# Order of a TensorE slot in the prompt attention: scores, values of unit n-3, projection piece, turns of unit n-2

## What is computed

```python
def mla_project(h, pos, w_in, q_norm, w_uq, kv_norm, w_uk):
    a = h @ w_in
    cq, ckv, kpe = jnp.split(a, [Q_LORA, Q_LORA + KV_LORA], axis=-1)
    q = (rmsnorm(cq, q_norm) @ w_uq).reshape(B, T, MLA_HEADS, QK_NOPE + QK_ROPE)
    ...
s = einsum(q, k) * MLA_SCALE                      # 16 heads, 96 wide (64 + 32 rotary)
s = jnp.where(kpos[None, :] <= qpos_b[:, None], s, -jnp.inf)
p = jax.nn.softmax(s, axis=-1)
o = p @ v                                         # 64 wide per head, then @ w_o
```

## Time and profile before

| what | value |
|---|---|
| median of 3 runs (lowest, highest) | 1759.67 us (1758.48, 1760.13) |
| the profiled execution, its own time | 1764.47 us |
| its span, first to last instruction | 1762.6 us |
| TensorE matmul busy | 1556.1 us, 88% of the span |
| VectorE, ScalarE, GpSimd busy | 757.0, 514.1, 389.0 us |
| mean granted TensorE clock | 0.92 of full speed |

### The profile page before, as it was taken

One profiled execution on the slowest core, in us unless ns is written; L12 is line 12 of the kernel. 1 busy time (PEld: TensorE's weight loads), 2 busy tenths in 40 slices (PEclk: granted clock), 3 DMA queues, 4 the chain that ended last, 5 costly groups with the idle time before them and its releaser, 6 DMA issues.

```text
span 1762.6 us, 28171 instructions
## 1 busy us (share of the span) xinstructions
PE 1556.1 (88%) x11027; PEld 1386.2 (79%) x11027; DVE 757.0 (43%) x1000; ACT 514.1 (29%) x884; POOL 389.0 (22%) x282
## 2 busy tenths in 40 slices
PE   3778998899995899999999489999976999999995
PEld 3635655666794899999999477778866999999994
DVE  5425665221137433334343744443546434343435
ACT  3125555221123212222122335443433212122221
POOL 4110000000025413223152500000036405050432
PEclk7989999888696899999999689999987999999996
DMA  7200000323020223222223222222220232232211
GB/s 178 87 16 1 1 1 1 81 72 85 2 72 24 72 85 89 88 85 83 83 83 84 62 60 89 77 88 72 83 72 24 86 94 84 85 91 86 83 59 51
DMA packets 210856, 119.99 MB, mean 68 GB/s; under 512 B 22118, under 2 KB 206592, under 8 KB 210784
## 3 DMA queue, kind: packets, MB, share of 16 engines
q1 hardware_dynamic: 206800, 105.73, 21.1%
q0 software_dynamic: 3984, 13.25, 2.3%
HBM read 111.37 MB, written 7.59 MB: 67 GB/s over the span
## 4 chain that ended last, share of the span: by engine, by line
PE 80%; DVE 11%; ACT 6%; issue 2%; POOL 1%; DMA 0%; DVEq 0%; ACTq 0%; POOLq 0%
PE ps L1523 56%; PE ps L1784 2%; DVE y L1109 2%; PE ps L1662 2%; DVE act_lo L1100 2%; PE ps L1547 2%; PE ps L1760 2%; PE ps L1746 1%; DVE rstd_post L1095 1%; PE ps L1698 1%; PE ps L1621 1%; POOL ssum L619 1%; PE ps L1762 1%; PE ps L1561 1%; DVE x L1114 1%
## 5 line engine op out<-in xcount | busy, mean ns | idle before, releaser
L724 ACT CAST w_hi<-w_raw 128x1024 fp32r<-128x1024 f32 x172 | 180.6, 1051 | 780.6 <-PE ps L1523 771.3
L1523 PE MATMUL ps<-act_hi,w_hi 128*128 128x280 f32 (+1 forms) x1504 | 319.9, 294 | 17.0 <-DVE w_lo L1090 14.2
L1523 PE MATMUL ps<-act_hi,w_lo 128*128 128x280 f32 (+1 forms) x1504 | 317.4, 292 | 0.0
L1523 PE MATMUL ps<-act_lo,w_hi 128*128 128x280 f32 (+1 forms) x1504 | 316.3, 292 | 0.0
L1090 DVE TENSOR_TENSOR w_lo<-w_raw,w_hi 128x1024 fp32r<-128x1024 f32 x172 | 254.9, 1482 | 47.5 <-ACT w_hi L724 45.6
L1523 PEld LDWEIGHTS ps<-act_hi,w_hi 128*128 128x128 f32 x1504 | 240.9, 191 | 23.3 <-DVE w_lo L1090 15.4
L1523 PEld LDWEIGHTS ps<-act_hi,w_lo 128*128 128x128 f32 x1504 | 241.3, 191 | 0.0
L1523 PEld LDWEIGHTS ps<-act_lo,w_hi 128*128 128x128 f32 x1504 | 240.2, 190 | 0.0
L1523 PE MATMUL ps<-h_hi,w_lo 128*128 128x280 f32 (+1 forms) x1024 | 213.7, 290 | 0.0
L1523 PE MATMUL ps<-h_hi,w_hi 128*128 128x280 f32 (+1 forms) x1024 | 212.9, 289 | 0.0
L1523 PE MATMUL ps<-h_lo,w_hi 128*128 128x280 f32 (+1 forms) x1024 | 212.7, 289 | 0.0
(11 more groups left out here) (294 smaller groups left out, 1961.0 us busy)
## 6 DMA issues: line engine op xcount, KB each, us to landing
w_raw<-in_mlp_w_up_dram SPq DMA_DIRECT2D x64, 512.0 KB, 4.1
w_raw<-in_mlp_w_down_dram SPq DMA_DIRECT2D x64, 512.0 KB, 3.6
w_raw<-in_gla_w_in_dram SPq DMA_DIRECT2D x24, 512.0 KB, 3.9
pg_ckv<-in_cache_ckv_dram SPq DMA_DIRECT2D x64, 128.0 KB, 2.0
w_raw<-in_mla_w_o_dram SPq DMA_DIRECT2D x8, 512.0 KB, 4.8
sts<-in_state_gla_dram POOLq DMA_DIRECT2D x4, 1024.0 KB, 6.4
out_dram<-sts POOLq DMA_DIRECT2D x4, 1024.0 KB, 5.1
w_raw<-in_gla_w_o_dram SPq DMA_DIRECT2D x8, 512.0 KB, 3.7
```

Source lines behind the costliest of these rows:

```text
L724: nc.scalar.copy(w_hi[g % SPLIT][:], w_raw[raw_slot(g)][:]).then_inc(w_rounded, 1)
L1523: last = nc.tensor.matmul(out[:, h, 0:n], w[:, c, :], a[:, c, t0 + n * h:t0 + n * h + n], start=(c == 0 and k == 0), stop=(c == DC - 1 and ...
```

## The change

In TensorE's loop over the slots the call of `pair_out(n - 3)` moves from the last place of the slot to the place right behind `scores(n)`, ahead of the piece and of `turn_probs(n - 2)`.

```diff
             for n in range(N_UNIT + 4):
                 if n < N_UNIT:
                     scores(n)
-                    if piece_at(n) is not None:
-                        piece(*piece_at(n))
+                if n >= 3 and out_at(n - 3) is not None:
+                    pair_out(n - 3)
+                if n < N_UNIT and piece_at(n) is not None:
+                    piece(*piece_at(n))
                 if 2 <= n < N_UNIT + 2:
                     turn_probs(n - 2)
-                if n >= 3 and out_at(n - 3) is not None:
-                    pair_out(n - 3)
```

## The result

The change is slower, by more than forecast. On the first chip the median of four runs is 1802.38 us against 1759.9 us for the kernel before; the ratio is 1.0237, with a 95% interval of 1.0219 to 1.0254. On a second chip the same two kernels gave 1799.05 and 1764.72 us, ratio 1.0177 (1.0149 to 1.0204). Forecast were 1786 us and 1774 to 1800; the first measurement lies outside. The direction held, the size didn't: +42 and +34 us by the medians, against +26.

What follows compares the result with a forecast made beforehand. TensorE was taken to set the attention's pace, so lost cover costs time: 17.0 (pairs 2, 4, 6) + 2.8 + 1.3 + 0 (odd pairs) = 21.1, plus 5 for clock falls, 26 us in all. Median near 1786 us, range 1774 to 1800.

Steps and rivals of the forecast that it cites:

- The slots of an even pair: Even pairs, pieces and turns uncovered: +0.46, +1.12, +2.4, +0.93, +0.75 in slots 1, 2, 4, 6, 8, together 5.66 us.
- slot 4: Even pairs: late QN1 delays VectorE's maximum and split, so unit 1's values start at 233.07; +2.4 us.
- Slot 8: Even pairs: unit 5's values wait for placement until 238.04, the turns formerly ahead began at 237.29; +0.75 us.
- Odd pairs: Values fill pieces' waits for bank 7, while slot 2 loses cover; net 0, between -1.0 and +0.5 us per pair.
- Pair 0: No values in slots 1 and 2; KN0's lost cover in slot 4 plus slots 6 and 8: +2.8 us.
- Pair 7: Issues no pieces; 0.46 + 0.12 + 0.75, giving +1.3 us.
- two new falls, +5: Stalls in slots 2 and 4 drop TensorE's clock to 1.2 GHz at two of ten places, 2.5 us each.
- rival 2: Many clock falls, five or more: 21 + 12.5 us and up, time 1793 and above; chance 0.15.
- L1701's wait: TensorE's wait of unit 8's values for VectorE's split, slot 2: grows from 7.2 to 12 to 13 us, 8 times.
- (3): Even pairs' slot 4: QN1 leaves its bank while TensorE is behind, only KN0's 1.08 us lost; 1777 without falls; chance 0.10.
- (4): Values fill pieces' bank-7 waits, odd pairs gain 1.6 us each, time 1755; shares 0.05 with no change.
- The saving of some 2 us: Weight loads pulled past a waiting one save about 0.2 us at each of 11 uncovered pieces; none counted.

Runs made afterwards that it cites:

- filled: The change plus 22 unused matmuls in the stalls of slot 2 (pairs 1 to 7) and slot 4 (pairs 0, 2, 4, 6); ratio 1.0079 to the kernel before.

## Why the prediction was wrong in size

In the means of three profiles each, the prompt attention went from 169.5 to 200.0 us (+30.5), the sample attention from 171.0 to 178.4 (+7.4), the rest from 1286.1 to 1286.6.

- **The bound** was right. TensorE sets the pace of the even pairs, and what stands ahead of the values was cover.
- **The slots of an even pair**: the table above. Slots 1, 2, 4 and 6 came within 0.04 us; slot 4, which hid best, is +2.44 against +2.4. **Slot 8** was too high, +0.49 for +0.75. The 0.75 was the spacing from the turns to the values, 237.29 to 238.04. The turns take 0.49 of it; for the rest TensorE stood still before, and an old wait is no new price. Slots 0, 3, 5 and 7, which began behind values and now begin behind turns, are 0.10 shorter each, which the sum didn't have and no run explains.
- **Odd pairs**: 0 predicted, -0.28 measured. **Pair 0**: +2.8 predicted, 2.1 measured (19.72 filled against 17.60, at nearly the same clock). **Pair 7**: +1.3 predicted; its best pair of profiles, 23.73 at 0.97 against 21.50 at 1.00, gives about 2.2. Together the order is 14.25 + 2.1 + 2.2 = 18.5 us, where the sum had 21.1: too large, by 2.6.
- **The clock** is the term that failed, "I take two new falls, +5". In the prompt attention it was 30.5 - 18.5 = 12 us. I had counted falls as single events with the price of the one in pair 7. In fact pairs 2, 4 and 6 lost 3.66 each (26.92 against 23.26): in pair 4 the clock stayed at 0.50 for 13.6 us, through the stalls of slots 2 and 4, and falls came in pair 1 and, as before, in pair 7. In the second profile of the change they sat elsewhere (pairs 3 and 5 with 27.3 us each, pairs 4 and 6 with 23.7 and 23.4), and pairs 1 to 6 took 153.5 us in all against 155.3. I had this case, as rival 2, at 0.15, and its price for the clock, 12.5 us and up, was near; its time, 1793 and above, still lacked the sample attention.
- **The sample attention** was left out entirely: "Nothing outside the stretch of 135 to 330 us changes". It gave +7.4 us. The profile of before showed its clock, 0.80 on the mean, below full, and the prediction didn't look at it. In the sum's own terms (order, clock, the rest of the kernel), 21.1 + 5 + 0 were forecast and about 18.5 + 12 + 7.4 measured. That the order came out 2.6 too high and so hid a part of what the clock lacked is luck.
- **What was to show it**: L1701's wait of 12 to 13 us came to 12.9; new waits of L1698 came, 2.3 us in pair 0's slot 4, shorter in even pairs because slow matmuls filled them; even pairs of 23 to 25 us came only where the clock was 0.93 or more; odd pairs were 24.4 at full clock, not 24.7.
- The rivals: the chain of slot 4 being short (3) is refuted by 2.44. The gain of the odd pairs (4) exists, 0.8 us a pair, but only where the values are ready; it is too small to time.
- The Trainium skill, page "TensorE: Matmul & The Clock Gate", section "Step-by-step: what each phase is for", says that weight loads are pulled ahead of matmuls in flight. The saving of some 2 us that the prediction weighed by it does not show: slot 2 cost 1.15, the full piece and turns, and in pair 4 of the change PEld, the weight loads, began for the values of unit 8 at 238.96 and for QN1 behind them at 240.28, 0.03 and 0.01 us before their matmuls.

## What to carry to other kernels

In a hand-ordered list, an instruction that waits for other engines belongs behind the work that fills its wait; compare its earliest start with what stands ahead of it, and follow each displaced producer one round further (here QN1 to the maximum to the next values). If the engine already stood still ahead of that instruction in the old order, this idle time is no part of the new price. If the move opens stalls on TensorE, price the clock by pair or by stage, not by single falls, and test it by filling the stalls with matmuls that nobody needs. Before calling a later stage unaffected, look at its clock in several profiles.

## What the runs showed of the hardware that was not expected

- Adding 22 unneeded matmuls made a kernel faster: the prompt attention took 186.7 us with the stalls filled and 197.7 to 201.3 without.
- A stall of 1.69 us and the matmuls of 16 columns behind it went with the lower clock in pairs 2, 4 and 6 in the first and third profile, but in the second profile of the same program pairs 3 and 5 were hit too, and pairs 4 and 6 less. Before, pair 7 fell in two of three profiles: 23.65 us at 0.86, and without the fall

```profile
282.34:303.84 21.50, 17.30 (x166) 11.18 (x164) 11.38 (x38) 11.76 (x40) 0.00 (x0) 1.00 0.01 2
```

  so that this fall cost 2.15 us, not the 2.5 that I took.
- The sample attention of one unchanged instruction list took from 165.5 us (the order piece, values, turns) to 178.5, with the granted clock from 0.81 to 0.74. That is 0.7% of the kernel, more than the gain of many a change, and one profile doesn't show it.
